# First layer norm of an encoder block: rows only centred and scaled ahead of TensorE's turning, gamma and beta applied afterwards per partition

## What is computed

```
proj   = x @ w_in                      # q, k, v, su, sv, gate_a, gate_b
merged = sig(ga) * (attention(q, k, v) @ w_na) + sig(gb) * (spatial_gating(su, sv) @ w_sg)
x      = layer_norm(alpha * x + merged @ w_out, ln1_g, ln1_b)      # the first layer norm
y_peer = peer(x)      # q = x @ wq; scores against two sets of 128 keys; top 16 of each and of their sums;
                      # sum over heads and picks of gelu(x . u[id]) * g * v[id]
x      = layer_norm(alpha * x + y_peer, ln2_g, ln2_b)

def layer_norm(x, g, b):
    y = (x - mean(x)) * rsqrt(var(x) + 1e-5)
    return y * g + b
```

## Time and profile before

| | |
|---|---|
| median of 3 runs | 1092.3 us (1091.41 to 1094.45) |
| the profiled execution's own time | 1092.07 us |
| its span from first to last instruction | 1090.2 us |
| mean granted TensorE clock | 0.974 of 2.4 GHz |
| busy share of the span: PE, DVE, ACT, POOL | 94%, 77%, 41%, 42% |
| chain that ended last, by engine | PE 45%, POOL 39%, issue 9%, DVE 3% |

### The profile page before, as it was taken

The page is one execution under the profiler, slowest core; times in us unless marked ns, Lnnn a source line. Parts: engine busy times, 40 slices in busy tenths (PEclk is TensorE's granted clock), DMA queues, the critical chain, the costliest instruction groups (busy, mean ns, idle before and its releaser), DMA issues.

```text
span 1090.2 us, 20494 instructions
## 1 busy us (share of the span) xinstructions
PE 1023.3 (94%) x6821; PEld 938.8 (86%) x6821; DVE 837.0 (77%) x1485; ACT 451.1 (41%) x649; POOL 452.8 (42%) x332
## 2 busy tenths in 40 slices
PE   8999999899999999999999999039999999999995
PEld 7878898899999999999999999028888888888884
DVE  4476467668999998988888887028888888888887
ACT  4384433344443344444444444014444444444442
POOL 3920000058888888788888888830000000000000
PEclk9999999999999999999999999559999999999998
DMA  9867688446666667877877775247787777777773
GB/s 312 256 247 251 216 291 293 156 108 125 147 136 135 138 148 164 188 170 159 177 169 172 167 163 96 0 126 236 241 242 238 241 244 237 241 243 240 242 241 124
DMA packets 146752, 210.42 MB, mean 193 GB/s; under 512 B 47392, under 2 KB 95328, under 8 KB 146720
## 3 DMA queue, kind: packets, MB, share of 16 engines
q1 hardware_dynamic: 109280, 208.58, 60.7%
q0 software_dynamic: 37440, 1.43, 10.1%
HBM read 192.00 MB, written 17.96 MB: 193 GB/s over the span
## 4 chain that ended last, share of the span: by engine, by line
PE 45%; POOL 39%; issue 9%; DVE 3%; DMA 2%; ACT 1%; SPq 0%; POOLq 0%; DVEq 0%; ACTq 0%
POOL expert_weights L460 38%; PE ps L1297 32%; PE ps L1214 10%; DMA w_raw<-in_w_in_dram 1%; POOL bias L437 1%; PE ps L1104 1%; DMA bias_raw<-in_na_rpb_dram 1%; ACT w_hi L583 1%; DVE w_lo L914 1%; PE ps L1082 0%; DVE xres L707 0%; DVE xres L714 0%; PE ps L1092 0%; DMA expert_weights<-gw,cell 0%; DVE small L695 0%
## 5 line engine op out<-in xcount | busy, mean ns | idle before, releaser
L460 POOL DMA_INDIRECT expert_weights<-gw,cell x256 | 413.0, 1613 | 246.9 <-DVE gw L901 166.3
L1255 PE MATMUL ps<-act_hi,uT_hi 128*128 128x256 f32 x1024 | 295.1, 288 | 0.0
L1255 PE MATMUL ps<-act_hi,uT_lo 128*128 128x256 f32 x1024 | 289.9, 283 | 0.0
L1255 PE MATMUL ps<-act_lo,uT_hi 128*128 128x256 f32 x1024 | 289.7, 283 | 0.0
L661 ACT ACTIVATE v_hi<-v_raw 128x512 fp32r<-128x512 f32 x256 | 147.9, 626 | 246.4 <-PE ps L1297 199.4
L1297 PE MATMUL ps<-v_hi,hid_hi 128*128 128x512 f32 x512 | 158.9, 392 | 45.0 <-DVE v_lo L992 45.0
L1255 PEld LDWEIGHTS ps<-act_lo,uT_hi 128*128 128x128 f32 x1024 | 196.6, 192 | 0.0
L1255 PEld LDWEIGHTS ps<-act_hi,uT_hi 128*128 128x128 f32 x1024 | 196.6, 192 | 0.0
L1255 PEld LDWEIGHTS ps<-act_hi,uT_lo 128*128 128x128 f32 x1024 | 196.3, 192 | 0.0
L992 DVE TENSOR_TENSOR v_lo<-v_raw,v_hi 128x512 fp32r<-128x512 f32 x256 | 164.8, 685 | 0.0
L1297 PE MATMUL ps<-v_lo,hid_hi 128*128 128x512 f32 x512 | 158.6, 391 | 0.0
(11 more groups left out here) (153 smaller groups left out, 1399.2 us busy)
## 6 DMA issues: line engine op xcount, KB each, us to landing
v_raw<-in_peer_v_dram SPq DMA_DIRECT2D x128, 512.0 KB, 4.2
u_raw<-in_peer_u_dram SPq DMA_DIRECT2D x68, 512.0 KB
u_raw<-in_peer_u_dram SPq DMA_DIRECT2D x240, 128.0 KB
w_raw<-in_w_in_dram SPq DMA_DIRECT2D x8, 2048.0 KB, 9.2
expert_weights<-zeros SPq DMA_DIRECT2D x16, 1024.0 KB, 12.0
g_in<-expert_weights SPq DMA_DIRECT2D x128, 128.0 KB, 3.1
w_raw<-in_peer_wq_dram SPq DMA_DIRECT2D x4, 2048.0 KB, 10.7
w_raw<-in_w_out_dram SPq DMA_DIRECT2D x2, 2048.0 KB, 9.3
```

The source lines that it names most:

```text
L460: pool.indirect_dma_start(out=table_cells, out_offset=bass.IndirectOffsetOnAxis(ap=cell[:, t, k:k + 1], axis=0), in_=gw[:, t, k:k + 1], in ...
L1255: ins = pe.matmul(ps[:, bank, 0:T], (uT_hi, uT_hi, uT_lo)[part][:, slot, k, :], (act_hi, act_lo, act_hi)[part][:, k, :], start=(k == 0 and ...
```

## The change

DVE no longer applies gamma and beta ahead of the turning. ACT computes nothing new before the square root; behind it, DVE inverts the standard deviation and makes `shift` = -mean/std of row block 1 (128 values); DVE then centres and scales row block 0 in one `tensor_scalar`, and ACT does row block 1 in one activation (Identity, scale 1/std, bias `shift`). PE turns both after 30 instead of 40 dummy transposes. After the turning, ACT applies gamma and beta as scale and bias per partition while it copies PSUM to a new tile `x1T` in eight activations of 256 columns; DVE makes `act_hi` by a copy and `act_lo` by a subtraction from `x1T`, per pair of column blocks. PE begins w0 at the first pair (w0's first half goes by k in two passes). The residual rows in `xres` still need gamma and beta: POOL applies them by four `tensor_tensor` operations of 1024 columns, after the eighth `act_lo` and ahead of the scatters. Two small DMAs load gamma and beta in the new layout. ACT (in half 33) and DVE (at the second layer norm) wait for POOL's four operations.

```diff
-NORMING = 40
+NORMING = 30
...
+                sp.dma_start(ln1gT, ln1_g[0].rearrange("(p k) -> p k", k=KD)).then_inc(s["ln1T_in"], 16)
+                sp.dma_start(ln1bT, ln1_b[0].rearrange("(p k) -> p k", k=KD)).then_inc(s["ln1T_in"], 16)
...
+        pool.wait_ge(s["ln1_in"], 32)
+        pool.wait_ge(s["act_lo_done"], 8)
+        for t in range(TB):
+            pool.tensor_tensor(xres[:, t, :], xres[:, t, :], ln1g[:], ALU.mult).then_inc(s["scaled"], 1)
+            pool.wait_ge(s["scaled"], t + 1)
+            pool.tensor_tensor(xres[:, t, :], xres[:, t, :], ln1b[:], ALU.add).then_inc(s["x1_ready"], 1)
 
         pool.wait_ge(s["zeroed"], 16 * ZERO_DMAS)
...
             if hc == NHC - 1:
+                act.wait_ge(s["x1_ready"], TB)
...
             if hc == HC["w0"]:
                 sqrt_var(1, TB)
-                split_act(1, 6)
+                act.wait_ge(s["shift_ready"], 1)
+                act.activation(xres[:, 1, :], xres[:, 1, :], ACT.Identity, bias=shift, scale=rstd[:, 1:2]) \
+                    .then_inc(s["second_normed"], 1)
+                act.wait_ge(s["ln1T_in"], 32)
+                for k in range(KD):
+                    act.wait_ge(s["tp_done"], 6 + k // 2 + 1)
+                    act.activation(x1T[:, k, :], ps[:, 4 + k // 2, k % 2 * T:(k % 2 + 1) * T], ACT.Identity,
+                                   bias=ln1bT[:, k:k + 1], scale=ln1gT[:, k:k + 1]).then_inc(s["x1T_done"], 1)
...
             if hc == HC["w0"]:
                 means_and_variances(2)
-                normed(1, xres, ln1g, ln1b, xres, s["x1_ready"], s["ln1_in"], [(t, 0, D) for t in range(TB)])
-                split_act(6, 4)
+                dve.wait_ge(s["ln_std"], 2)
+                ch.step(dve.reciprocal(rstd[:, 0:TB], rstd[:, 0:TB]))
+                ch.wait()
+                dve.scalar_tensor_tensor(shift, mv[:, 2:3], -1.0, rstd[:, 1:2], ALU.mult, ALU.mult) \
+                    .then_inc(s["shift_ready"], 1)
+                dve.tensor_scalar(xres[:, 0, :], xres[:, 0, :], mv[:, 0:1], rstd[:, 0:1], ALU.subtract,
+                                  ALU.mult).then_inc(s["first_normed"], 1)
+                for g in range(4):
+                    hi = act_hi[:, 2 * g:2 * g + 2, :]
+                    dve.wait_ge(s["x1T_done"], 2 * g + 2)
+                    dve.tensor_copy(hi, x1T[:, 2 * g:2 * g + 2, :]).then_inc(s["act_hi_done"], 1)
+                    dve.wait_ge(s["act_hi_done"], 4 + g + 1)
+                    dve.tensor_tensor(act_lo[:, 2 * g:2 * g + 2, :], x1T[:, 2 * g:2 * g + 2, :], hi.bitcast(F32),
+                                      ALU.subtract).then_inc(s["act_lo_done"], 1)
...
+        dve.wait_ge(s["x1_ready"], TB)
         for t in range(TB):
             dve.wait_ge(*((s["y_first"], 1), (s["y_done"], NB))[t])
...
-                if name == "w0":
-
-                    pe.wait_ge(s["act_lo_done"], 6 if first else 8)
+                if name == "w0" and not first:
+                    pe.wait_ge(s["act_lo_done"], 8)
...
-                for m, ks in [(m, range(KW)) for m in columns_of] if hc else \
+                for m, ks in [(m, range(KW)) for m in columns_of] if hc not in (0, HC["w0"]) else \
                         [(m, range(k, k + KW // 2)) for k in (0, KW // 2) for m in columns_of]:
...
+                    if hc == HC["w0"] and m == 0:
+                        pe.wait_ge(s["act_lo_done"], 5 + ks.start // 2)
...
-                transpose_rows([(s["x1_ready"], t + 1) for t in range(TB)], free_banks)
+                transpose_rows([(s["first_normed"], 1), (s["second_normed"], 1)], free_banks)
```

More of the change, by code:

```diff
@@ L166, in hybrid_block @@
     ln1b = sb("ln1b", [P, D], 181 * K1)
+    x1T = sb("x1T", [P, KD, T], 129 * K1)
     sk_raw = sb("sk_raw", [P, 2, P], 203 * K1)
@@ L207, in hybrid_block @@
     ln2b = sb("ln2b", [P, D], 29 * K1)
-    small = sb("small", [P, 88], 207 * K1)
+    small = sb("small", [P, 104], 207 * K1)
     stats = small[:, 0:24]
@@ L220, in hybrid_block @@
     column = small[:, 84:86]
+    shift = small[:, 86:87]
+    ln1gT = small[:, 88:96]
+    ln1bT = small[:, 96:104]
     ps = nc.psum_tensor("ps", [P, 8, 512], F32).__enter__()
@@ L240, in hybrid_block @@
              "yna_lo_done", "mix_done", "sgln_done", "ysg_done", "ysgT_done", "ysgT_hi_done",
-             "ysgT_lo_done", "merged_sum", "mrg_hi_done", "mrg_lo_done", "ln_var", "ln_std", "x1_ready",
+             "ysgT_lo_done", "merged_sum", "mrg_hi_done", "mrg_lo_done", "ln_var", "ln_std", "shift_ready", "first_normed", "second_normed", "x1T_done", "scaled", "x1_ready", "ln1T_in",
              "act_hi_done", "act_lo_done", "pq_first", "pqT_first", "key_scores", "sc_copied", "soft_in", "soft_exp", "route_done",
```

## The result

The changed kernel takes 1098.07 us, the median of 16 runs (1092.78 to 1100.20); the kernel before, run beside it, 1091.82. The ratio is 1.005, with a 95% interval of 1.0037 to 1.0063: slower by some 5.4 us by the ratio (6.25 between the two medians), where 2.4 us less had been forecast. The profiled execution took 1095.5 us, its span 1093.7 us, 3.4 and 3.5 more than before. It is the second fastest of the sixteen, so it shows less of the loss than the medians do. In this profile the loss can be laid out stage by stage.

What follows compares the result with a forecast made beforehand. PE was busy 94%, but GpSimd's scatters, following the first route, were taken to set the end. The profiled 1092.07 us minus the front's 2.4, all else 0, gave 1089.7 us; range 1087.2 to 1093.0.

Steps and rivals of the forecast that it cites:

- That the end moves one to one with `route(0)`: Scatters: kernel's end shifts as much as the first route, 226 to 223.6, if POOL is free and later batches stay early.
- the four rivals: Whole kernel: POOL first, -2.4 us (0.50); DVE first, -4.4 or -2.8 (0.32); slower, to 1097 (0.08); no change (0.10).
- The front: Stretch up to the first scatter: w0's second half starts at 201.65 instead of 204.03, a gain of 2.4 us.
- PE's start behind the root: Start of w0: PE begins at 193.8, 2.7 us before 196.48, with the root ending at 188.89.
- VectorE's pass over block 0: Behind the root: one tensor_scalar over 1024 columns takes 0.75 us, or 1.15 at one column per step.
- Identity behind the root: ACT's activation over block 1: 1.24 us, hidden; a table load, if needed, adds 1.3 us, some 0.9 showing.
- The race for the lock: After the eighth `act_lo`: POOL starts at 196.9, ahead of DVE's `w_lo` of half 27 at 197.05, by 0.15 us.
- Rival B: Lock at half 27: DVE goes first, PE has no wait; -4.4 us at full clock, -2.8 at lower; chance 0.32.
- Rival C: Lock at half 27: POOL keeps DVE out between its operations; all four in a row give 1097 us; chance 0.08.
- That who comes second waits for the whole instruction of the first: POOL against DVE: the two exclude each other; POOL's operation of 2.4 us holds `w_lo` from 197.0 to 199.4.
- The clock: PE in w0's first half: full clock holds (6 in 10), ending at 199.6; otherwise 201.2.
- GpSimd is free before `route(0)`: Ahead of the scatters: POOL done by about 211.4, `route(0)` at 223.6, 12 us of cover.

Runs made afterwards that it cites:

- e4: The kernel before, plus GpSimd's four tensor_tensor operations of 1024 columns on a spare tile ahead of the scatters; 1098.13 us, ratio 1.0056.
- e1: The changed kernel without GpSimd's four tensor_tensor operations and the two waits for them; 1087.01 us, ratio 0.9954 to the kernel before.
- f4: The kernel before, plus four one-input tensor_scalar operations of 1024 columns on GpSimd ahead of the scatters; 1093.31 us, ratio 1.0018.
- e3: The changed kernel with its six new semaphores declared behind all others, so the scatters' keep their old numbers; 1096.55 us, ratio 1.0039 to the kernel before.
- e7: The changed kernel, but VectorE applies gamma and beta to the residual rows while waiting for the scatters; 1088.15 us, ratio 0.9973 to the kernel before.
- f3: The kernel before, plus eight tensor_tensor operations of 512 columns on GpSimd right behind the masks; 1104.30 us, ratio 1.0122.
- f1: The kernel before, plus one tensor_tensor of 1024 columns on GpSimd ahead of the scatters; 1099.18 us, ratio 1.0067.
- g3: The kernel before, plus one tensor_tensor of 128 columns on GpSimd ahead of the scatters; 1098.78 us, ratio 1.0046.

## Why the prediction was wrong, point by point
- *That the end moves one to one with `route(0)`* was the sentence that failed, in its silent half: "All behind it is unchanged work". The instructions are unchanged, but the 256 scatters take 6.45 us longer in the profile. None of the four rivals holds this. The sum needed a term "256 times the change of one scatter"; it was put at nothing, without a reason. The runs show it as more than the whole loss: +6.1 us when the four operations alone are added (e4), and with them alone taken away (e1) scatters of 1545 ns and a time 5.0 us below before. At 256 in a row on the bounding engine, 15 ns make 3.8 us by themselves, and the rest comes from single longer scatters.
- *The front* was right in mechanism and nearly in size. The forecast of 2.4 compared 201.65 with 204.03, but 204.03 is the end of the first half's last matmul; the second half's first starts at 203.81, so like for like 2.2 was forecast. Measured: 2.03 from the root to w0's second half and 1.96 to the first scatter; the profile's 2.33 holds 0.37 that isn't the change's. PE's start behind the root: 4.91 forecast, 5.00 measured. VectorE's pass over block 0: 0.75 forecast (its own terms, 0.35 + 768 * 0.00049, give 0.73), 0.81. Eight activations at 0.45: 3.7 forecast, 3.75. Identity behind the root needed no table load (the gap of 0.43 ahead of L632 is VectorE's).
- *The race for the lock* went to GpSimd, by 0.04 us (196.72 against 196.76). One operation: 2.4 forecast, 2.40 measured, a choice near the top of the bounds 1.26 and 2.5 that no row had forced. `w_lo`: about 4.5 forecast, 4.50. Rival B's worth is in e1: 4.1 us from the root on (4.4 forecast). Rival C is refuted: VectorE came in between the first and the second and again between the second and the third, which took 4.31 and 4.43 for it.
- *That who comes second waits for the whole instruction of the first* held for GpSimd's two-input operations, but not in general: in f4 `w_lo` started 0.6 us behind a one-input `tensor_scalar` of 2.8 us and still took only 2.60.
- *The clock* held in this execution, and e3 has the other case; that both end in the same second half was confirmed to 0.01 us. What the forecast didn't allow for is that the old front can run at the full clock too. In e4, which has the old front, the granted clock stayed at 1.00 there, and the second half starts 13.54 us behind the root's end (203.14 - 189.60), so against this execution the changed front leads by 0.65 us only, and e1's by 2.7.
- *GpSimd is free before `route(0)`*: it idled 14.14 us ahead of the first scatter (12 forecast).

Through the whole, -5.0 us (e1, with neither collision nor slow scatters) plus 2.1 us (collision) plus 6.1 us (e4) gives +3.2, and the measurement is +5.4 (4.0 to 6.9); the intervals of e1 and e4, about 2 us each way, allow for the difference, but I can't say that nothing else is in it.

What stays open is the cause inside GpSimd. The runs show what sets the slower state, and that neither 160.9 us of idling nor a select ends it; they don't show what it is. What a scatter does in its 1545 ns isn't visible in these traces.

## What to carry to other kernels
Where one instruction is repeated hundreds of times on the bounding engine, its own duration belongs among the things that a change may alter: compare its median before and after, even if nobody touched it. Work is not free on an idle engine when that engine later sets the end; here the engine with real slack was VectorE, idle for 47.62 us in the same wait (PE for 44.17). And a wait in which the bounding engine's partner idles is the place to put deferred work, which e7 did with four instructions and two loads that wait for that moment.

## What was not expected of the hardware
- A single GpSimd `tensor_tensor` of 64 or more float32 columns (322 ns) raises the median of the later indirect DMAs of the same program from 1545 to 1560 or 1561 ns, and five to nine of 256 take over 2.5 us instead of none to three; after eight of 512 columns it was still so behind 160.9 us of idling (f3). After one of 8 columns, or four in the one-input form, it was 1552 to 1553 ns, with times 0.12 to 0.18% above before.
- GpSimd's two-input operation took 2.40 us for 1024 float32 columns on 128 partitions (2368 ns in f1) and 0.46 us for 128 (g3), VectorE's for 1024 took 1.22 to 1.23 us. GpSimd's one-input `tensor_scalar` of 1024 columns was slower than its two-input one, 2771 ns at the least, and its `affine_select` took 1042 ns.
- The one-input `tensor_scalar` of GpSimd and VectorE's `w_lo` shared f4's time unevenly: with GpSimd first, `w_lo` took 2.60 us instead of 2.29; with `w_lo` first, GpSimd's operation took 4874 ns.
